# A two-layer diffusion backbone: how the attention transposes its probabilities and multiplies them with the values

## The reference

```python
def block(qi):                      # qi: 128 queries
    s = jnp.einsum('bkgqd,bksd->bkgqs', qi, k).astype(F32) * scale
    p = jax.nn.softmax(s, axis=-1).astype(v.dtype)
    return jnp.einsum('bkgqs,bkse->bkgqe', p, v)
```

## Time and profile before

| what | value |
|---|---|
| time, median of 3 runs (lowest, highest) | 4398.51 us (4389.56, 4407.89) |
| span of the profiled execution | 4394.2 us |
| time of the profiled execution | not given apart; the median lies 4.3 us above its span |
| TensorE matmuls busy | 3875.4 us, 88% of the span, 20738 instructions |
| TensorE weight loads busy | 3242.2 us, 74% |
| VectorE busy | 2214.8 us, 50% |
| ScalarE busy | 1264.1 us, 29% |
| GpSimd busy | 795.6 us, 18% |

### The profile page before, as it was taken

The page is one execution under the profiler, slowest core; times in us unless marked ns, Lnnn a source line. Parts: engine busy times, 40 slices in busy tenths (PEclk is TensorE's granted clock), DMA queues, the critical chain, the costliest instruction groups (busy, mean ns, idle before and its releaser), DMA issues. The chain is left out here.

```text
span 4394.2 us, 54314 instructions
## 1 busy us (share of the span) xinstructions
PE 3875.4 (88%) x20738; PEld 3242.2 (74%) x20738; DVE 2214.8 (50%) x2872; ACT 1264.1 (29%) x1962; POOL 795.6 (18%) x315
## 2 busy tenths in 40 slices
PE   7999659959978999999999799669689789999997
PEld 6788537838866888888888488538578657777775
DVE  1402555455424465565566601555455336666666
ACT  2222124445423222222221311134445232222222
POOL 0233000000021334334322111000000113222331
PEclk9999779979989999999999899779899899999998
DMA  4233220010031122212210122210100201111111
GB/s 174 79 108 110 70 75 1 7 47 7 7 115 45 53 62 72 67 62 72 68 37 24 40 97 81 79 51 6 42 6 5 82 30 52 48 43 43 43 54 42
DMA packets 106326, 242.03 MB, mean 55 GB/s; under 512 B 10656, under 2 KB 54944, under 8 KB 106080
## 3 DMA queue, kind: packets, MB, share of 16 engines
q1 hardware_dynamic: 97712, 232.14, 16.2%
q10 hardware_dynamic: 8496, 8.26, 0.6%
HBM read 200.39 MB, written 39.98 MB: 55 GB/s over the span
## 5 line engine op out<-in xcount | busy, mean ns | idle before, releaser
L108 POOL TENSOR_TENSOR wlo<-raw,whi 128x1024 fp32r<-128x1024 f32 x267 | 679.5, 2567 | 2474.4 <-ACT whi L97 2474.1
L1600 DVE SCALAR_TENSOR_TENSOR xT<-down_acc,mod,xT 128x512 f32<-128x512 f32 (+1 forms) x880 | 560.2, 695 | 281.5 <-PE down_acc L138 279.0
L136 PE MATMUL up_acc<-h_hi,whi 128*128 128x512 f32 (+1 forms) x1760 | 655.7, 373 | 37.8 <-POOL wlo L108 18.8
L137 PE MATMUL up_acc<-h_lo,whi 128*128 128x512 f32 (+1 forms) x1760 | 649.5, 369 | 0.0
L138 PE MATMUL up_acc<-h_hi,wlo 128*128 128x512 f32 (+1 forms) x1760 | 648.8, 369 | 0.0
L97 ACT ACTIVATE whi<-raw 128x1024 fp32r<-128x1024 f32 x267 | 281.1, 1055 | 587.8 <-PE down_acc L138 412.8
L136 PEld LDWEIGHTS up_acc<-h_hi,whi 128*128 128x128 f32 x1760 | 332.7, 189 | 102.8 <-ACT up L1519 45.6
L138 PEld LDWEIGHTS up_acc<-h_hi,wlo 128*128 128x128 f32 x1760 | 332.5, 189 | 56.2
L137 PEld LDWEIGHTS up_acc<-h_lo,whi 128*128 128x128 f32 x1760 | 332.9, 189 | 53.5 <-issue 0.2
L652 DVE TENSOR_REDUCE negmax<-scores 128x1 f32<-128x1280 f32 (+1 forms) x180 | 247.1, 1373 | 214.0 <-PE scores L538 213.8
L136 PE MATMUL proj_acc<-h_hi,whi 128*128 128x512 f32 (+1 forms) x936 | 340.7, 364 | 15.7 <-DVE h_lo L335 15.7
(11 more groups left out here) (205 smaller groups left out, 6391.9 us busy)
## 6 DMA issues: line engine op xcount, KB each, us to landing
raw<-in_w_mlp SPq DMA_DIRECT2D x180, 512.0 KB, 3.6
raw<-in_w_proj SPq DMA_DIRECT2D x63, 512.0 KB, 4.2
proj_scratch<-stage SPq DMA_DIRECT2D x33, 640.0 KB, 3.3
raw<-in_w_mix SPq DMA_DIRECT2D x24, 512.0 KB, 4.4
kc<-proj_scratch SPq DMA_DIRECT2D x38, 192.0 KB, 2.7
ada_raw<-in_w_ada SPq DMA_DIRECT2D x10, 512.0 KB, 7.6
xT<-in_xT SPq DMA_DIRECT2D x1, 5120.0 KB, 21.8
o_raw<-mix_scratch SPq DMA_DIRECT2D x8, 640.0 KB, 4.9
```

Source lines behind the costliest of these rows:

```text
L108: nc.gpsimd.tensor_tensor(self.lo[k][:, :], self.raw[k][:, :], self.hi[k][:, :].bitcast(f32), ALU.subtract).then_inc(self.lo_ready, 1)
L136: nc.tensor.matmul(out, hi, xhi, start=start, stop=False)
L137: nc.tensor.matmul(out, hi, xlo, start=False, stop=False)
L1600: nc.vector.scalar_tensor_tensor(xs, db[g % DB][:, :w], mod_of(layer, 5, m, c), xs, ALU.mult, ALU.add).then_inc(added, 1)
```

## The change

- Steps of all pairs are numbered through, `n` from 0 to N-1, and every program is written out without a loop. Two steps (a group `G = n // 2`) are two neighbouring query blocks of one head.
- The transposes of `probs` go into the columns of the score tile that held the scores of the same step, in three pieces by bank (blocks 0 to 3, 4 to 7, 8 and 9).
- ScalarE copies each piece, rounded to f32r, into `pth` (the high part), VectorE subtracts it from the piece in PSUM into `ptl` (the low part). Scores of step n+2 wait, piece by piece, for VectorE's subtraction (`lo_done`).
- The values are prepared once, `vs`: per head and block 128 columns, 64 of the high part and 64 of the low part, f32r; stationary. The moving operand is 256 query columns of `pth`, then of `ptl`. The result is 128 rows (high and low) by 256 queries in a bank `O`. ScalarE copies it to `osb`, two f32 products with `fold` (two stacked identities of 64) add the halves and turn it to queries by 64, VectorE scales it by 1/sum.
- The flush of a pair is spread over steps of the next pair, two blocks at a time, from `FLUSH0` = 3 steps after the pair's end, through columns 1280 to 1535 of the score tile and two buffers of `o_feat`; that of the last pair comes behind the last step.
- Low parts of queries and keys are made by GpSimd, and the grouped queries are doubled by DMAs within SBUF on SP's queue.
- In the first scopes the low parts of the values are made by VectorE out of PSUM, in ten operations (latent) and six (grouped), and ScalarE's three copies of the grouped values become six.

The diff, cut to its core:

```diff
@@ attention @@
+        heads = list(range(XB if last else 0, BLK))
+        NH = len(heads)
+        NS = 2 * NH
+        N = npairs * NS
+        NP = NH // 2
+        NG = N // 2
+        FLUSH0 = 3
-        pt = s.sb("pt", [P, BLK, P])
+        pth = [s.sb(f"pth{i}", [P, BLK, 256], f32r) for i in range(2)]
+        ptl = [s.sb(f"ptl{i}", [P, BLK, 256], f32r) for i in range(2)]
+        osb = [s.sb(f"osb{i}", [P, 256]) for i in range(2)]
+        o_feat = s.sb("o_feat", [P, 2, 256])
-        T = psum_banks(s, "probsT", 2)
+        O = psum_banks(s, "values", 2)
...
+        def pieces(n):
+            return [(0, 2)] if is_ctx(n) else [(0, 4), (4, 8), (8, 10)]
+        cut = [sum(len(pieces(x)) for x in range(n)) for n in range(N + 1)]
+        def flush_of(n):
+            f = n - NS - FLUSH0
+            return (f // NS, f % NS) if f >= 0 and f % NS < NP and f // NS < npairs else None
 @block.tensor
+            def scores(n):
+                ...
+                for p, (k0, k1) in enumerate(pieces(n)):
+                    if n >= 2:
+                        ...
+                            pe.wait_ge(lo_done, cut[n - 2] + p + 1)
+                    c0, w = k0 * P, (k1 - k0) * P
+                    for x, (q, k) in enumerate(terms[hd]):
+                        mm = nc.tensor.matmul(S[n % 2][:, c0:c0 + w], q[:, b * P:(b + 1) * P], k[:, c0:c0 + w],
+                                              start=(x == 0), stop=(x == len(terms[hd]) - 1))
+                mm.then_inc(s_done, 1)
+            def transposes(n):
+                pe.wait_ge(exp_done, n + 1)
+                for k0, k1 in pieces(n):
+                    if k0 == 8 and flush_of(n):
+                        flush(n)
+                    for b in range(k0, k1):
+                        tr = nc.tensor.transpose(S[n % 2][:, b * P:(b + 1) * P], probs[n % 2][:, b * P:(b + 1) * P], ident[:, :])
+                    tr.then_inc(t_done, 1)
...
+            def values(G, pt, done, n_done, end):
+                n = 2 * G
+                pe.wait_ge(done, n_done)
+                nk = 2 if is_ctx(n) else BLK
+                for k in range(nk):
+                    mm = nc.tensor.matmul(O[G % 2][:, :256], values_of(n // NS, head_of(n), k), pt[G % 2][:, k, :],
+                                          start=(not end and k == 0), stop=(end and k == nk - 1))
...
+            for n in range(N + FLUSH0 + NP):
+                if n < N:
+                    transposes(n)
+                elif flush_of(n):
+                    flush(n)
+                G = n // 2 - 1
+                if 0 <= G < NG:
+                    if n % 2 == 0:
+                        if G >= 2:
+                            pe.wait_ge(o_done, G - 1)
+                        values(G, pth, hi_done, cut[2 * G + 2], False)
+                    else:
+                        values(G, ptl, lo_done, cut[2 * G + 2], True)
+                if n % 2 == 0 and 0 <= G - 1 < NG:
+                    fold_halves(G - 1)
+                if n + 2 < N:
+                    scores(n + 2)
 @block.scalar
+            def flush(n):
+                ...
+                act.wait_ge(flush_t, u + 1)
+                if u >= 2:
+                    act.wait_ge(stored[u % 2], 16 * (u // 2))
+                nc.scalar.activation(o_feat[:, u % 2, :], S[n % 2][:, TOK:TOK + 256], ACT.Copy).then_inc(flushed, 1)
+            exp(0)
+            for n in range(N + FLUSH0 + NP):
+                if n < N:
+                    high(n)
+                if flush_of(n):
+                    flush(n)
+                if n + 1 < N:
+                    exp(n + 1)
+                if n % 2 == 1 and 0 <= n // 2 - 1 < NG:
+                    evacuate(n // 2 - 1)
 @block.vector
+            def low(n):
+                ...
+                for p, (k0, k1) in enumerate(pieces(n)):
+                    dve.wait_ge(hi_done, cut[n] + p + 1)
+                    if k0 == 8 and flush_of(n):
+                        ...
+                        dve.wait_ge(flushed, g * NP + f + 1)
+                    nc.vector.tensor_tensor(ptl[G % 2][:, k0:k1, j * P:(j + 1) * P],
+                                            S[n % 2][:, k0 * P:k1 * P].rearrange("p (b q) -> p b q", q=P),
+                                            pth[G % 2][:, k0:k1, j * P:(j + 1) * P].bitcast(f32), ALU.subtract).then_inc(lo_done, 1)
...
+            for n in range(N + FLUSH0 + NP):
+                if n + 1 < N:
+                    maximum(n + 1)
+                if n < N:
+                    low(n)
+                if n % 2 == 0 and 0 <= n // 2 - 2 < NG:
+                    normalise(n // 2 - 2)
+                if n < N and n % NS == 2:
+                    prep(dve, n // NS, 1)
+                if n < N and n % NS == NH + 2 and n // NS + 1 < npairs:
+                    prep(dve, n // NS + 1, 0)
 @block.gpsimd
+            for g in range(npairs):
+                for hd in range(2):
+                    if g:
+                        pool.wait_ge(s_done, (g - 1) * NS + (hd + 1) * NH)
+                    prep_pool(pool, g, hd)
@@ latent_attention @@
+                    for b in range(BLK):
+                        dve.wait_ge(evac, nv + b + 1)
+                        nc.vector.tensor_tensor(vs[:, :, b, HD:], banks[(nv + b) % 4][:, :MH * HD].rearrange("p (h x) -> p h x", x=HD),
+                                                vs[:, :, b, :HD].bitcast(f32), ALU.subtract).then_inc(v_low, 1)
...
+                def prep(dve, g, hd):
+                    nc.vector.tensor_scalar(qh[hd][:, c0:], of(q_all, g, hd, c0), 1.0, None, ALU.mult).then_inc(high_made, 1)
+                    nc.vector.tensor_scalar(kh[hd][:, :], of(k_all, g, hd, 0), 1.0, None, ALU.mult).then_inc(high_made, 1)
@@ grouped_attention @@
+                def prep_double(sp, g, hd):
+                    r, other = halves(hd)
+                    sp.wait_ge(high_made, 2 * g + hd + 1)
+                    sp.dma_start(qh[hd][other, q0:].bitcast(f32), qh[hd][r, q0:].bitcast(f32)).then_inc(doubled[hd], 16)
+                    sp.wait_ge(low_made, 2 * g + hd + 1)
+                    sp.dma_start(ql[hd][other, q0:].bitcast(f32), ql[hd][r, q0:].bitcast(f32)).then_inc(doubled[hd], 16)
```

More of the change, by code:

```diff
@@ L506, in attention @@
-        flush_t, flushed, stored = s.sem("flush_t"), s.sem("flushed"), s.sem("stored")
-        o_tok_read = s.sem("o_tok_read")
-        block = s.enter_context(nc.Block())
-        def is_ctx(i):
-            return blocks[i][1] < XB
-        na = [sum(1 if is_ctx(x) else 2 for x in range(i)) for i in range(NS + 1)]
-        nb = [sum(0 if is_ctx(x) else 1 for x in range(i)) for i in range(NS + 1)]
-        fblocks = list(range(XB if last else 0, BLK))
-        fgroups = [fblocks[i:i + 4] for i in range(0, len(fblocks), 4)]
@@ L517, in attention @@
[L517 to L531 removed]
+        t_done, hi_done, lo_done = s.sem("t_done"), s.sem("hi_done"), s.sem("lo_done")
@@ new lines, in attention, with head_of, block_of, is_ctx @@
+        pv_done, osb_done, fold_done, o_done = s.sem("pv_done"), s.sem("osb_done"), s.sem("fold_done"), s.sem("o_done")
+        own, folder = s.sem("own"), s.sem("folder")
+        flush_t, flushed = s.sem("flush_t"), s.sem("flushed")
+        stored = [s.sem(f"stored{i}") for i in range(2)]
+        block = s.enter_context(nc.Block())
+        def head_of(n):
+            return (n % NS) // NH
+        def block_of(n):
+            return heads[n % NH]
+        def is_ctx(n):
+            return block_of(n) < XB
@@ L542, in scores @@
-            def scores(g, i):
-                if i == 0 or blocks[i][0] != blocks[i - 1][0]:
-                    prep_wait(pe, g, blocks[i][0])
-                if is_ctx(i):
-                    score_columns(i, 0, CTX).then_inc(s_done, 1)
-                else:
-                    score_columns(i, 0, 512)
-                    score_columns(i, 512, 512)
-                    score_columns(i, 1024, 256).then_inc(s_done, 1)
-            def transposes(i, dst, b0, b1, done):
-                for b in range(b0, b1):
-                    tr = nc.tensor.transpose(dst[:, (b - b0) * P:(b - b0 + 1) * P], probs[i % 2][:, b * P:(b + 1) * P], ident[:, :])
-                tr.then_inc(done, 1)
@@ new lines, in transposes @@
+            def transposes(n):
[7 more added lines that the diff above has]
+            def flush(n):
+                g, f = flush_of(n)
+                pe.wait_ge(o_done, g * 2 * NP + NP + f + 1)
+                if n >= N:
+                    pe.wait_ge(lo_done, cut[N])
+                    pe.wait_ge(flushed, max(g * NP + f - 1, 1))
+                for j in range(2):
+                    b = heads[2 * f + j]
+                    tr = nc.tensor.transpose(S[n % 2][:, TOK + j * P:TOK + (j + 1) * P], o_tok[:, b, :], ident[:, :])
+                tr.then_inc(flush_t, 1)
@@ new lines, in values, with fold_halves @@
+            def values(G, pt, done, n_done, end):
[5 more added lines that the diff above has]
```

(30 more changed lines are left out.)

278 lines of the change are left out of this document (101 added, 177 removed).

## The result

The changed kernel takes 4251.16 us (median of 4 runs, 4249.89 to 4252.16) for 4397.6 before (4 runs, 4389.56 to 4407.89): ratio 0.9668, interval 0.9654 to 0.9683. The forecast was 4288, the range 4230 to 4345. The profiled execution took 4252.16 us with a span of 4250.3; the span before was 4394.2. So 143.9 us of the span went, where I had booked 111.

A forecast was written before the change was run, and what follows sets the result against it. TensorE was taken to bound the attention stages. Steps gain 133 us and boundaries 23; flushes cost 5, preparation 11, starts 17.6, ends 11: net 111, span 4394.2 to 4283, plus 4.3 makes 4288 us; range 4230 to 4345.

The forecast's parts named there:

- Who sets a step: In full steps, odd ones wait for VectorE's subtraction (4.44 us latent, 3.92 grouped); the fold makes even ones 4.52 and 3.96.
- Full steps: 64 latent and 96 grouped full steps, shorter by 0.88 and 0.80 us each, were to give 133 us.
- The allowance of 0.05 us a step for handoffs: Added to each full step because handoffs cross three engines three times a step, each with a wait.
- the reciprocal: VectorE's small operation between maximum and subtraction in each step, charged 0.2 us with its gap.
- Boundaries, flushes, preparation: Between pairs and heads: 23 us gained from boundaries, 5 lost to flushes in later steps, 11 to preparation on VectorE.
- Starts: Ahead of each stage's first scores, the exposed first head and the values' low parts were to cost 17.6 us together.
- Ends: After each stage's last step, the last pair's flush through two buffers was to cost 11 us over the four stages.
- 1 (handoffs longer): Rival for the full steps: handoffs cost more than allowed, steps of 4.8 and 4.35 us, 4339 us; chance 0.20.
- 2 (TensorE's sums reached): Rival: VectorE's handoffs overlap, steps reach TensorE's 4.3 and 3.75 us, starts half as dear, 4234 us; chance 0.12.
- 3 (subtraction slowed by GpSimd): Rival: VectorE's subtraction slows to 2.57 ns a column, steps take 5.85 us, 4550 us; chance 0.04.
- 4 (clock): Rival: the clock falls to 1.2 GHz in the steps, as transposes don't count as busy; all steps so, 4875; chance 0.02.
- The 4.3 us between span and median: The old median of 4398.5 lay 4.3 us above the profiled span; the same was added to the new span.

The follow-up runs named there:

- e1: The changed kernel with one more VectorE operation, a maximum over 512 columns read from PSUM, ahead of the first subtraction in each full step: 4331.8 us.
- e2: The changed kernel with three more TensorE transposes ahead of the third piece in each odd full step: 4264.32 us.
- e3: The changed kernel with three more TensorE transposes ahead of the third piece in each even full step: 4269.14 us.
- e5: The kernel before the change, without the flush of a pair of heads except the last pair of each stage: 4379.9 us, for 4397.6 before.
- e4: The kernel before the change with probabilities and values rounded to f32r and no low parts, so ten product instructions instead of twenty: 4282.3 us, for 4397.6 before.
- e6: The changed kernel with each stage's first head prepared without SP's queue: VectorE makes a low part, ScalarE doubles the grouped queries: 4245.66 us.

## Why the prediction was right, and where its sizes were off

- **Who sets a step: right.** VectorE in odd steps, TensorE in even ones (e1, e2, e3). Only the piece was wrong: in grouped steps I had the third piece decide; the second does, and the third is through at 3157.07, 0.29 us before its scores start.
- **Full steps: the mis-sized term.** Booked 133 us. From the lengths of 4.25 and 4.47, 3.81 and 3.89 it is 64 × 1.05 + 96 × 0.94 = 157 (4.36 and 3.85 as means, 5.41 and 4.79 before). Three sizes make the 24 us. The allowance of 0.05 us a step for handoffs was 8 us for nothing. The odd steps are 0.19 us (latent) and 0.11 (grouped) shorter than booked, 11 us, and in the latent ones this is the reciprocal: it was charged 0.2 us of VectorE's path and costs nothing there, since the maximum started at 739.56 and the subtraction 1.48 later (741.04); so from the start of the last scores matmul to the next scores it is 2.53 us (739.24 to 741.77) for 2.75. The even steps are 0.05 and 0.07 shorter, 5 us. The durations I had bounded held, by shape in the changed kernel (count, busy us, mean ns):

```profile
L674 DVE TENSOR_TENSOR ptl<-scores,pth 128x512 fp32r<-128x512 f32 x320 | 203.5, 678 | 12.9 <-ACT pth L629 12.9
...
L674 DVE TENSOR_TENSOR ptl<-scores,pth 128x256 fp32r<-128x256 f32 x180 | 74.7, 415 | 4.0 <-ACT pth L629 4.0
```

  678 and 415 ns for 690 and 420. TensorE's terms were each a little off and made up for each other: from the last scores matmul to the product 1.14 us (743.50 to 744.64) for 1.22, the ten product instructions 1.28 to the fold for 1.15, and the fold's four 0.36 to the next scores for 0.46, 2.78 in all for 2.83.
- **Boundaries, flushes, preparation: 7 booked, about 14 measured** (171.6 − 157). e5 gives the boundaries 21.3, so everything else cost about 7, not 16. A flush costs 0.22 us in an even step and nothing in an odd one, where TensorE has room: 12 such steps, 2.6 us for the 5 booked. The 11 us for preparation were too much, as the steps after a change of head show a few tenths at most. The short steps, booked at nothing, are in the 7 too: ten steps around a change of head in layer 0, two of them short, went from 47.68 to 40.05 us latent and from 42.96 to 35.60 grouped, 0.8 and 0.2 us less than eight plain steps would gain.
- **Starts: 17.6 booked, 17.2 measured, the parts right within 1.3 us.** Order of time of the changed kernel, first the latent start of layer 1:

```profile
2874.06 0.68 DVE L895 TENSOR_SCALAR mqh<-mq 96x1024 fp32r<-96x1024 f32 x1
2874.66 0.82 DVE L896 TENSOR_SCALAR mkh<-mk 96x1280 fp32r<-96x1280 f32 x1
2874.82 2.85 POOL L901 TENSOR_TENSOR mql<-mq,mqh 96x1024 fp32r<-96x1024 f32 x1 [224.07 <-DVE mqh L895]
2877.64 2.87 POOL L903 TENSOR_TENSOR mkl<-mk,mkh 96x1280 fp32r<-96x1280 f32 x1
2880.65 0.77 PE L554 MATMUL scores<-mkh,mqh 96*128 96x512 f32 x1 [7.94 <-POOL mkl L903]
```

  and the grouped one of layer 0, with the DMA that doubles the low part:

```profile
911.72 2.87 POOL L1012 TENSOR_TENSOR gql<-gq,gqh 64x1280 fp32r<-64x1280 f32 x1 [135.05 <-DVE gqh L1007]
914.61 0.50 SPq L1019 DMA_DIRECT2D gql<-gql  x1
917.94 0.55 PE L554 MATMUL scores<-ks,gqh 128*128 128x256 f32 x1 [35.13 <-DMA gql<-gql]
```

  The total is right partly by luck: latent 6.59 us in layer 1 for the 6.05 forecast, grouped 6.10 for 6.05 though the transfer takes longer than the 2.6 I took, and what comes ahead of the preparation, the values' low parts, 1.0 us for the 2.3 booked in the grouped stage of layer 1 (4.0 in all, less 3.0). In the latent start the keys' operation was right (2.87 us for 2.95), the queries' was not: 1024 columns took 2.85 us for the 2.4 booked. VectorE makes the keys' high part beside it; in the grouped stages, where it doesn't, an operation of 1024 columns takes 2.33 us at least. No run takes the two apart. Landing times of these transfers (min, median, max, us):

```profile
L1019 SPq DMA_DIRECT2D gql<-gql x12: 461/462/500, 914.6 to 3242.1; - x12
...
DMA to landing us min/median/max: 2.8/3.1/3.6
```

- **Ends: 11 booked, 9.9 measured.** Two buffers for the output make the last portions wait for a store, as forecast. Order of time of the changed kernel, end of the latent stage of layer 1, ScalarE:

```profile
3032.81 0.69 ACT L638 ACTIVATE o_feat<-scores 128x256 f32<-128x256 f32 x2 [3.80 <-DMA mix_scratch<-o_feat]
```

- **Rivals.** 1 (handoffs longer) is out: steps are shorter than forecast. 2 (TensorE's sums reached) is half right: TensorE's own work sets the even steps, 4.47 where its sum with all of the fold in that step is 4.5; the odd ones stay on VectorE, and the starts cost what was booked. The first piece came 0.22 us sooner, as this rival had it (0.15), and the time, 4251, lies nearer to its 4234 than to the 4288 of the forecast. 3 (subtraction slowed by GpSimd) is out: none of the 500 subtractions out of PSUM took over 693 ns, those beside GpSimd included. 4 (clock) is out: 1.00 in every stage of the changed kernel behind its first steps; it was the kernel before that had steps at 0.50.
- **The 4.3 us between span and median** were not a property of the kernel: in the profiled execution after the change the time is 1.9 above the span, and the rest of the 4.3 was the difference between two runs. It moved the forecast by 2 us.

## What to carry to other kernels

Before moving work off the busiest engine, write the new chain out from one start to the next for each kind of step: here halving TensorE's product instructions was the larger part (113 of 172 us by e4), and the rest hung on which engine came last. Cost a small operation between two long ones from the gap between the long ones, not from its own length, and book a handoff once. Room found in one kind of step is taken only where no other work already uses it: count flush and short steps apart before multiplying.

## What the runs showed of the hardware

- **VectorE waits for GpSimd, it isn't slowed in proportion.** In e6 GpSimd's operation ends at 670.76 and VectorE's, with both inputs in SBUF, at 672.11, 1.35 later; in layer 1 GpSimd ends at 2881.01 (2878.16 + 2.85) and VectorE at 2882.36 (2878.85 + 3.51), again 1.35 later. Alone it takes 1.48. Both fit a VectorE that stood still until GpSimd was through. The Trainium skill, SBUF — State Buffer, section SBUF: two separate sides, says that the pair of ports shared by GpSimd and a VectorE operation with two SBUF inputs is an exclusive lock which the one that starts first holds for its whole instruction; both starts agree with it. By that, rival 3's price per column from the earlier trace rows would be such a wait and no rate, which no run tested; the subtraction with an input in PSUM stayed at 693 ns or less. The Trainium skill, VectorE: DVE Perf Modes, section Two Vector instructions with no wait between them, which the prediction names for two SBUF inputs, also counts an operation in a 2-port mode as a user of the interface shared with GpSimd; the 2.85 us of GpSimd's 1024 columns beside VectorE's making of the keys' high part (0.82 us for 1280 columns) would fit it, but no run here tests it.
- **The clock stayed up with a larger share of transposes.** From the first transpose to the product it is 1.01 us of the 3.85 of a grouped step (of 4.79 before), and the clock was 0.99 over that stage. The Trainium skill, TensorE: Matmul & The Clock Gate, Part 4: PE-mode transpose, would have them not count as busy; at this share it changed nothing here, and no run with a larger share was made.
- A small operation can vanish: the 0.15 us reciprocal lies between a maximum of 1.49 us and a subtraction that starts 1.48 after the maximum did.
